# An order of two conversions at the start, and eight moves per weight tile spread over three groups

## The chip, the cores and the metric

One core of one Trainium2 chip runs the whole kernel. The metric is the device time of one execution in microseconds (us), the median of the timed runs.

## The reference

One decoder layer on 512 tokens of width 2048, in float32. Its input is multiplied by one wide weight; seven parts of the product go into a causal convolution of 31 taps with a layer norm and a gate, and into a forgetting attention of 16 heads with a gate. Both halves go through one output weight, and a residual with a layer norm ends it.

```python
z = jnp.einsum("bsd,de->bse", h, w_in) + b_in
glu_val, glu_gate, gate_c, q, k, v, f_logit, gate_a = _split_columns(z)
y_conv = _conformer_conv(glu_val, glu_gate, w_dw, b_dw, g_cn, b_cn)
y_conv = y_conv * jax.nn.silu(gate_c)
y_attn = _forgetting_attention(q, k, v, f_logit)
y_attn = y_attn * jax.nn.silu(gate_a)
y = jnp.concatenate([y_conv, y_attn], axis=-1)
sub = jnp.einsum("bse,ed->bsd", y, w_out) + b_out
h = _layer_norm(DN_ALPHA * h + sub, g_post, b_post)
```

## The kernel before

**Products.** Both large products are done in float32r with operands split into a high and a low half, three matmuls for one (`mm3`, lines 1081 to 1083), and by Strassen-Winograd's scheme: seven products of half-sized blocks instead of eight. A *group* g is 128 columns of two parts of the input product; there are 56, three for each of the 16 heads and 8 for the last gate. A group has seven *units* m of 24 matmuls each. They run in the order 1, 2, 5, 6, 3, 7, with unit 4 of a group in the third slot of the next one. So a step of the loop over (g, s) on each engine stands for one slot s of seven.

**Weights.** Of each group, SyncE (SP) loads four blocks of 512 KB into `raw` (`loads`, line 427): B11, B12, B21, B22. The seven units need B11, B21, B22, B12+B22 (unit 7, an adding DMA that GpSimd issues, `sum_3`, line 660, semaphore t3_in), B11+B12 (unit 5, `sum_1` on VectorE, line 1344, t1_done), that plus B22 (unit 6, `sum_2`, line 1352), and that plus B21 (unit 4, `sum_4`, an adding DMA, line 667, t4_in). For each unit n, ScalarE writes the high half (`high(n)`, line 801) and VectorE the low half (`low(n)`, line 1333) into one of three slots of `whl`; high(n) needs unit n-3 to be done.

**Start.** x is transposed on TensorE in quarters and sums of quarters, and split likewise by `x_high(f)` (ScalarE, line 808) and `x_low(f)` (VectorE, line 1379), four pieces of 512 columns each. Before the loop VectorE's order is low(0), a difference, low(1), a difference, sum_1(0), a difference (line 1403), low(2), x_low(3). ScalarE's is x_high(1), high(0), high(1), x_high(3), high(2), then three small copies of biases (lines 830 to 832). Unit n = 2 is group 0's unit 5, the third product that runs; it reads factor 3 of x. GpSimd's sum of x12 and x21 (line 717) waits for low_done 3, so for low(2).

**Sums of output weights.** The output product (behind group 55) needs, for each of 16 tiles k, four sums T1 to T4 of blocks of the output weight. They are built in DRAM (`t_dram`, 512 KB each) while the groups run: SP copies a block or an earlier sum (`copies`, `copy_sum`, line 482), and GpSimd adds another with an adding DMA (`out_sums`, `add_sum`, line 692). T1 and T3 start from w_out, T2 from a copy of the finished T1, T4 from a copy of the finished T2. Eight moves per tile. SP runs `loads(g)`, then `copies(g)`, then bias rows of the next head (four DMAs, line 510) and stores. `loads(g)` waits for low halves of groups g-2 and g-1, and, ahead of B22, for t3_in of g-1. So SP's step g is carried out while group g-1 is computed. GpSimd's step g is sum_3(g), masks, sum_4(g), out_sums(g).

**Other work.** VectorE carries the 31 taps of the convolution, some in each slot (`TAPS_AT`, and `TAPS_LAST` from group 48 on, line 1440). ScalarE's `evict` (line 867) takes unit 5 from PSUM behind the conversion of the same slot; TensorE's unit 3 waits for it. VectorE's eviction in slot 0 is line 1481; unit 4 waits for it.

Of the kernel before, what the change touches and what calls it, by code (L numbers as in the profile page):

```python
# [11 lines left out]
P = 128  # L12
SEQ = 512
D = 2048
# [3 lines left out]
HEADS = D // P  # L18
# [66 lines left out]
T1, T2, T3, T4 = range(4)  # L85
# [72 lines left out]
def build(nc, x, w_in, b_in, w_dw, b_dw, g_cn, b_cn, w_out, b_out, g_post, b_post, out, scratch):  # L158
# [3 lines left out]
    t_dram = nc.dram_tensor("out_sums_dram", (4, HEADS, P, 1024), F32).ap()  # L162
    ctx = ExitStack()
    with ctx:
# [205 lines left out]
        t_added = [sem(f"t{n + 1}_added") for n in range(4)]  # L370
# [52 lines left out]
        def _(sp):  # L423
# [57 lines left out]
            def copy_sum(t, k, src, copied):  # L481
                sp.dma_start(t_dram[t, k, :, :], src).then_inc(copied, 16)

            def copies(g):

                if g % 3 == 0 and 0 <= g // 3 - 2 < HEADS:
                    k = g // 3 - 2
                    sp.wait_ge(t_added[T1], 16 * (k + 1))
                    if k:
                        sp.wait_ge(t2_copied, 16 * k)  # L490
                    copy_sum(T2, k, t_dram[T1, k, :, :], t2_copied)
                if g % 3 == 1 and 0 <= g // 3 - 3 < HEADS:
                    k = g // 3 - 3
                    sp.wait_ge(t_added[T2], 16 * (k + 1))
                    if k:
                        sp.wait_ge(t4_copied, 16 * k)
                    copy_sum(T4, k, t_dram[T2, k, :, :], t4_copied)
                if g % 3 == 0 and 0 <= g // 3 - 1 < HEADS:
                    k = g // 3 - 1
                    if k:  # L500
                        sp.wait_ge(t13_copied, 32 * k)
                    copy_sum(T1, k, w_out[D + P * k:D + P * (k + 1), 0:1024], t13_copied)
                    copy_sum(T3, k, w_out[D + P * k:D + P * (k + 1), 1024:], t13_copied)

            def load_bias(h):

# [82 lines left out]
            g = GROUPS - 1  # L589
# [56 lines left out]
        def _(pool):  # L646
# [38 lines left out]
            def add_sum(t, k, src):  # L685
                if k:
                    pool.wait_ge(t_added[t], 16 * k)
                if t in (T1, T3):
                    pool.wait_ge(t13_copied, 32 * (k + 1))
                else:  # L690
                    pool.wait_ge(t2_copied if t == T2 else t4_copied, 16 * (k + 1))
                nc.gpsimd.dma_start(t_dram[t, k, :, :], src, accum_op=ALU.add).then_inc(t_added[t], 16)  # L692

            def out_sums(g):

                if g % 3 == 0 and 0 <= g // 3 - 1 < HEADS:
                    k = g // 3 - 1
                    add_sum(T1, k, w_out[D + P * k:D + P * (k + 1), 1024:])
                if g % 3 == 1 and 0 <= g // 3 - 1 < HEADS:
                    k = g // 3 - 1  # L700
                    row = P * CONV_ORDER[k]
                    add_sum(T3, k, w_out[row:row + P, 1024:])
                if g % 3 == 1 and 0 <= g // 3 - 3 < HEADS:
                    k = g // 3 - 3
                    row = P * CONV_ORDER[k]
                    add_sum(T4, k, w_out[row:row + P, 0:1024])
                if g % 3 == 2 and 0 <= g // 3 - 2 < HEADS:
                    k = g // 3 - 2
                    row = P * CONV_ORDER[k]
                    add_sum(T2, k, w_out[row:row + P, 1024:])  # L710
# [50 lines left out]
        def _(act):  # L761
# [17 lines left out]
            def high(n):  # L779

                if n not in UNIT_OF:
                    out_high(OUT_OF[n])
                    return
                g, m = UNIT_OF[n]
                if m == 1:
                    act.wait_ge(block_in[B11][g % 2], parity(g))
                elif m == 2:
                    act.wait_ge(block_in[B21][g % 2], parity(g))
                elif m == 3:
                    act.wait_ge(block_in[B22][g % 2], parity(g))  # L790
                elif m == 4:
                    wait_t4(act, g)
                elif m == 5:
                    act.wait_ge(t1_done, g + 1)
                elif m == 6:
                    act.wait_ge(t2_done, g + 1)
                else:
                    act.wait_ge(t3_in[g % 2], parity(g))
                if n >= 3:
                    act.wait_ge(unit_done, n - 2)  # L800
                nc.scalar.activation(w_high(n), source(n), ACT.Copy).then_inc(high_done, 1)  # L801

            def x_high(f):

                at_f = 4 * X_ORDER.index(f)
                for b in range(4):
                    act.wait_ge(xt_turned, X_BANKS if f == 2 else at_f + b + 1)
                    nc.scalar.activation(xh[:, f, 2 * b:2 * b + 2, :].rearrange("p k t -> p (k t)"), ps[:, x_bank(at_f + b), :],
                                         ACT.Copy, scale=-1.0 if f == 6 else 1.0).then_inc(xh_done, 1)
# [14 lines left out]
            x_high(1)  # L824
            high(0)
            high(1)
            x_high(3)
            high(2)
            act.wait_ge(rows_turned, 1)
            nc.scalar.activation(cols[:, :], ps[:, R5, 0:7 * HEADS], ACT.Copy).then_inc(cols_done, 1)  # L830
            nc.scalar.activation(cn[:, :], ps[:, R5, P:P + 3 * HEADS], ACT.Copy).then_inc(cols_done, 1)
# [1055 lines left out]
```

## Time and profile before

| | us |
|---|---|
| median of the timed runs | 1575.6 |
| all three | 1576.14, 1575.6, 1575.55 |
| the profiled execution | 1574.57 |
| its span, first to last instruction | 1572.8 |
| TensorE busy in it | 1549.7 |
| VectorE busy | 1445.4 |
| ScalarE busy | 840.9 |
| GpSimd busy | 250.3 |

PE is TensorE's matmuls, DVE VectorE, ACT ScalarE, POOL GpSimd, SP SyncE; "SPq" is SP's queue, whose instructions wait for semaphores and issue DMAs. L801 is line 801 of the kernel. Matmuls are pipelined, so the duration of one is longer than its share of the engine, and the starts tell the rate. An engine's idle time costs nothing unless TensorE comes to wait for it.

### The profile page before, as it was taken

Reading aid. Unit: us, or ns where it says so; the run is one execution under the profiler, and the core shown is the slowest. Engines: PE = TensorE matmul, PEld = TensorE weight load, DVE = VectorE, ACT = ScalarE, POOL = GpSimd, SP = SyncE. Lnnn points to the kernel's source line nnn. Section 1 sums busy time; section 2 is a strip of 40 time slices with the busy share of each in tenths; the row PEclk is TensorE's granted clock in tenths of the full one; section 3 lists DMA queues with packets and bytes.
Section 4 is the critical chain, followed back from the end, with each engine's and each line's share of the span. In section 5 each row is a group of like instructions: output and inputs, shape, how many; then the busy total and the mean of one; then the engine's idle time right before and its main releaser. Section 6 shows DMA issues by size and latency. Waiting matters only on the chain.

```text
span 1572.8 us, 29452 instructions
## 1 busy us (share of the span) xinstructions
PE 1549.7 (99%) x11574; PEld 1486.9 (95%) x11574; DVE 1445.4 (92%) x1975; ACT 840.9 (53%) x1225; POOL 250.3 (16%) x275
## 2 busy tenths in 40 slices
PE   7999999999999999999999999999999999999997
PEld 6999999999999999999999999999999988888886
DVE  7779999999999999999999999999989889986787
ACT  4565454554545545455454554545456676644462
POOL 1111212122121221212212122121110000000000
PEclk9999999999999999999999999999999999999999
DMA  8588888999999999999999999999899899888876
GB/s 226 127 204 190 222 204 215 234 211 241 224 226 229 213 241 223 231 217 223 239 219 232 223 220 238 230 224 219 196 278 287 245 345 340 297 235 249 259 211 204
DMA packets 316473, 365.23 MB, mean 232 GB/s; under 512 B 14561, under 2 KB 254337, under 8 KB 315025
## 3 DMA queue, kind: packets, MB, share of 16 engines
q1 hardware_dynamic: 285024, 259.93, 53.7%
q0 software_dynamic: 26784, 98.58, 35.0%
q10 hardware_dynamic: 4528, 4.85, 0.9%
q8 instruction: 92, 1.51, 0.4%
q14 instruction: 45, 0.37, 0.1%
HBM read 287.25 MB, written 87.06 MB: 238 GB/s over the span
## 4 chain that ended last, share of the span: by engine, by line
PE 90%; DVE 7%; issue 1%; DMA 1%; ACT 1%; SPq 0%; DVEq 0%; ACTq 0%
PE ps L1081 29%; PE ps L1083 29%; PE ps L1082 29%; DVE whl L1333 2%; DVE c_tiles L1440 1%; PE ps L1198 1%; DMA f_raw<-in_w_in_dram 1%; DVE raw L1352 1%; DMA raw<-in_w_out_dram 1%; PE ps L1192 0%; PE ps L1147 0%; ACT whl L801 0%; DVE xl L1379 0%; DVE raw L1344 0%; DVE res L1827 0%
## 5 line engine op out<-in xcount | busy, mean ns | idle before, releaser
L1081 PE MATMUL ps<-xh,whl 128*128 128x256 f32 x3136 | 894.4, 285 | 3.9 <-DVE xl L1379 1.4
L1083 PE MATMUL ps<-xh,whl 128*128 128x256 f32 x3136 | 887.7, 283 | 0.0
L1082 PE MATMUL ps<-xl,whl 128*128 128x256 f32 x3136 | 887.6, 283 | 0.0
L801 ACT ACTIVATE whl<-raw 128x1024 fp32r<-128x1024 f32 x392 | 415.3, 1061 | 555.2 <-PE ps L1083 474.6
L1081 PEld LDWEIGHTS ps<-xh,whl 128*128 128x128 f32 x3136 | 599.5, 191 | 5.9 <-issue 2.2
L1082 PEld LDWEIGHTS ps<-xl,whl 128*128 128x128 f32 x3136 | 599.7, 191 | 0.5 <-issue 0.5
L1083 PEld LDWEIGHTS ps<-xh,whl 128*128 128x128 f32 x3136 | 599.5, 191 | 0.0
L1333 DVE TENSOR_TENSOR whl<-raw,whl 128x1024 fp32r<-128x1024 f32 x392 | 477.5, 1218 | 52.4 <-ACT whl L801 52.4
L1440 DVE SCALAR_TENSOR_TENSOR c_tiles<-ps,taps,c_tiles 128x511 f32<-128x511 f32 (+14 forms) x480 | 349.9, 729 | 6.7
L660 POOL DMA_DIRECT2D raw<-raw x56 | 49.4, 883 | 558.3 <-DMA raw<-in_w_in_dram 452.1
L1081 PE MATMUL ps<-whl,yh 128*128 128x512 f32 x320 | 124.8, 390 | 1.3 <-issue 0.9
L1336 DVE TENSOR_TENSOR whl<-raw,whl 128x1024 fp32r<-128x1024 f32 x80 | 97.7, 1222 | 30.0 <-ACT whl L777 29.8
L1083 PE MATMUL ps<-whl,yl 128*128 128x512 f32 x320 | 124.6, 389 | 0.0
L1082 PE MATMUL ps<-whl,yh 128*128 128x512 f32 x320 | 124.6, 389 | 0.0
L777 ACT ACTIVATE whl<-raw 128x1024 fp32r<-128x1024 f32 x80 | 84.6, 1057 | 74.3 <-PE ps L1083 72.7
L667 POOL DMA_DIRECT2D raw<-raw x51 | 43.3, 848 | 319.9 <-DVE whl L1333 319.9
L1352 DVE TENSOR_TENSOR raw<-raw 128x1024 f32<-128x1024 f32 x56 | 73.8, 1319 | 1.9
L1081 PEld LDWEIGHTS ps<-whl,yh 128*128 128x128 f32 x320 | 60.1, 188 | 14.6 <-DVE whl_more L1336 1.7
L1083 PEld LDWEIGHTS ps<-whl,yl 128*128 128x128 f32 x320 | 60.1, 188 | 12.5
L1082 PEld LDWEIGHTS ps<-whl,yh 128*128 128x128 f32 x320 | 60.1, 188 | 12.4
L692 POOL DMA_DIRECT2D out_sums_dram<-in_w_out_dram x64 | 69.2, 1208 | 0.0
L1344 DVE TENSOR_TENSOR raw<-raw 128x1024 f32<-128x1024 f32 x56 | 68.2, 1218 | 0.0
(197 smaller groups left out, 1540.0 us busy)
## 6 DMA issues: line engine op xcount, KB each, us to landing
raw<-in_w_in_dram SPq DMA_DIRECT2D x224, 512.0 KB, 8.0
raw<-raw POOLq DMA_DIRECT2D x107, 512.0 KB, 6.0
out_sums_dram<-in_w_out_dram POOLq DMA_DIRECT2D x64, 512.0 KB, 9.6
raw<-out_sums_dram SPq DMA_DIRECT2D x64, 512.0 KB, 5.1
raw<-in_w_out_dram SPq DMA_DIRECT2D x48, 512.0 KB, 5.6
out_sums_dram<-in_w_out_dram SPq DMA_DIRECT2D x32, 512.0 KB, 9.4
out_sums_dram<-out_sums_dram SPq DMA_DIRECT2D x32, 512.0 KB, 9.7
x<-in_x_dram SPq DMA_DIRECT2D x8, 512.0 KB, 8.0
```

Of the source, the lines that this page charges most:

```text
L660: nc.gpsimd.dma_start(raw[:, ring(g, B12), :], raw[:, ring(g, B22), :], accum_op=ALU.add) \
L692: nc.gpsimd.dma_start(t_dram[t, k, :, :], src, accum_op=ALU.add).then_inc(t_added[t], 16)
L777: nc.scalar.activation(out_w(u, 0), raw_out(u), ACT.Copy).then_inc(high_done, 1)
L801: nc.scalar.activation(w_high(n), source(n), ACT.Copy).then_inc(high_done, 1)
L1081: nc.tensor.matmul(o, ah, bh, start=start, stop=False, skip_group_check=True)
L1082: nc.tensor.matmul(o, ah, bl, start=False, stop=False, skip_group_check=True)
L1083: return nc.tensor.matmul(o, al, bh, start=False, stop=True, skip_group_check=True)
L1333: vec.tensor_tensor(w_low(n), source(n), w_high(n), ALU.subtract).then_inc(low_done, 1)
L1336: vec.tensor_tensor(out_w(u, 1), raw_out(u), out_w(u, 0), ALU.subtract).then_inc(low_done, 1)
L1344: vec.tensor_tensor(raw[:, ring(g, SUM), :], raw[:, ring(g, B11), :], raw[:, ring(g, B12), :], ALU.add).then_inc(t1_done, 1)
L1352: vec.tensor_tensor(o, o, raw[:, ring(g, B22), :], ALU.add).then_inc(t2_done, 1)
L1440: vec.scalar_tensor_tensor(out=o[:, n:], in0=ps[:, U_BANK, 0:SEQ - n], scalar=tap, in1=o[:, n:], op0=ALU.mult, op1=ALU.add) \
```

## The change

Two things. On ScalarE, the conversion of unit 2's weights, high(2), is put ahead of the conversion of x's factor 3, x_high(3). And the eight moves of a tile are spread anew. Copies on SP in the steps g = 0, 1, 2 modulo 3 were T2, T1, T3 / T4 / none, and are T4, T2 / T3 / T1. GpSimd's additions were T1 / T3, T4 / T2 and are T1 / T4 / T3, T2. T1's copy of tile k now stands in step 3k+2 instead of 3k+3, T3's in 3k+4 instead of 3k+3, T4's in 3k+9 instead of 3k+10; T3's addition in 3k+5 instead of 3k+4. The semaphore of the copies of T1 and T3, which is shared, is waited for at 16 and 32 above each tile's start instead of 32.

```diff
             def copies(g):
 
+                if g % 3 == 0 and 0 <= g // 3 - 3 < HEADS:
+                    k = g // 3 - 3
+                    sp.wait_ge(t_added[T2], 16 * (k + 1))
+                    if k:
+                        sp.wait_ge(t4_copied, 16 * k)
+                    copy_sum(T4, k, t_dram[T2, k, :, :], t4_copied)
                 if g % 3 == 0 and 0 <= g // 3 - 2 < HEADS:
                     k = g // 3 - 2
                     sp.wait_ge(t_added[T1], 16 * (k + 1))
                     if k:
                         sp.wait_ge(t2_copied, 16 * k)
                     copy_sum(T2, k, t_dram[T1, k, :, :], t2_copied)
-                if g % 3 == 1 and 0 <= g // 3 - 3 < HEADS:
-                    k = g // 3 - 3
-                    sp.wait_ge(t_added[T2], 16 * (k + 1))
-                    if k:
-                        sp.wait_ge(t4_copied, 16 * k)
-                    copy_sum(T4, k, t_dram[T2, k, :, :], t4_copied)
-                if g % 3 == 0 and 0 <= g // 3 - 1 < HEADS:
+                if g % 3 == 1 and 0 <= g // 3 - 1 < HEADS:
                     k = g // 3 - 1
+                    sp.wait_ge(t13_copied, 32 * k + 16)
+                    copy_sum(T3, k, w_out[D + P * k:D + P * (k + 1), 1024:], t13_copied)
+                if g % 3 == 2 and g // 3 < HEADS:
+                    k = g // 3
                     if k:
                         sp.wait_ge(t13_copied, 32 * k)
                     copy_sum(T1, k, w_out[D + P * k:D + P * (k + 1), 0:1024], t13_copied)
-                    copy_sum(T3, k, w_out[D + P * k:D + P * (k + 1), 1024:], t13_copied)
...
                 if t in (T1, T3):
-                    pool.wait_ge(t13_copied, 32 * (k + 1))
+                    pool.wait_ge(t13_copied, 32 * k + (16 if t == T1 else 32))
...
                     add_sum(T1, k, w_out[D + P * k:D + P * (k + 1), 1024:])
-                if g % 3 == 1 and 0 <= g // 3 - 1 < HEADS:
+                if g % 3 == 2 and 0 <= g // 3 - 1 < HEADS:
                     k = g // 3 - 1
                     row = P * CONV_ORDER[k]
                     add_sum(T3, k, w_out[row:row + P, 1024:])
...
             high(1)
+            high(2)
             x_high(3)
-            high(2)
```

## Rows read from the trace of the kernel before

**Rows 1.** The page, span and part 1: busy us, share, instructions.

```profile
span 1572.8 us, 29452 instructions
PE 1549.7 (99%) x11574; PEld 1486.9 (95%) x11574; DVE 1445.4 (92%) x1975; ACT 840.9 (53%) x1225; POOL 250.3 (16%) x275
```

**Rows 2.** Busy time by stage (PE PEld DVE ACT POOL); then clock, DMA share, GB/s.

```profile
50.00:1100.00 1050.00, 1050.00 (x8659) 1045.70 (x8658) 997.19 (x1413) 553.82 (x856) 213.88 (x232) 1.00 0.93 220
1100.00:1160.00 60.00, 57.98 (x472) 56.89 (x471) 57.22 (x70) 26.51 (x35) 9.77 (x10) 1.00 0.92 227
```

**Rows 3.** Timeline of ACT at the start: start, us, instruction, idle before.

```profile
24.12 2.06 ACT L808 ACTIVATE xh<-ps 128x512 fp32r<-128x512 f32 x4 [6.39 <-PE ps L1147]
26.05 1.08 ACT L801 ACTIVATE whl<-raw 128x1024 fp32r<-128x1024 f32 x1
```

**Rows 4.** Timeline of DVE in the same stretch.

```profile
22.57 1.22 DVE L1344 TENSOR_TENSOR raw<-raw 128x1024 f32<-128x1024 f32 x1
23.70 2.28 DVE L1403 SCALAR_TENSOR_TENSOR x<-x 128x2048 f32<-128x2048 f32 x1
27.16 1.23 DVE L1333 TENSOR_TENSOR whl<-raw,whl 128x1024 fp32r<-128x1024 f32 x1 [1.17 <-ACT whl L801]
28.30 2.48 DVE L1379 TENSOR_TENSOR xl<-ps,xh 128x512 fp32r<-128x512 f32 x4
30.70 3.50 DVE L1352 TENSOR_TENSOR raw<-raw 128x1024 f32<-128x1024 f32 x1
```

**Rows 5.** Timeline of PE there.

```profile
29.13 0.35 PE L1081 MATMUL ps<-xh,whl 128*128 128x256 f32 x1 [1.44 <-DVE xl L1379]
...
34.95 0.52 PE L1147 MATMUL ps<-ident,x 128*128 128x128 f32 x3 [0.97 <-DVE xl L1379]
```

**Rows 6.** Timeline of POOL there.

```profile
28.54 4.58 POOL L717 TENSOR_TENSOR x<-x 128x2048 f32<-128x2048 f32 x1 [2.23 <-DVE whl L1333]
```

**Rows 7.** Timeline of PE in group 50.

```profile
1144.20 0.39 PE L1081 MATMUL ps<-xh,whl 128*128 128x256 f32 x1 [1.06 <-ACT p L867]
```

**Rows 8.** ACT at that moment; then, of its waits over the span (us, times, longest), one.

```profile
1142.73 1.06 ACT L801 ACTIVATE whl<-raw 128x1024 fp32r<-128x1024 f32 x1 [3.11 <-DMA raw<-raw]
...
ACT whl L801 <- DMA raw<-in_w_in_dram: 4.8, 2, 4.0
```

**Rows 9.** Timeline of POOL in groups 49 and 50.

```profile
1119.20 2.01 POOL L692 DMA_DIRECT2D out_sums_dram<-in_w_out_dram  x2
1134.27 0.88 POOL L660 DMA_DIRECT2D raw<-raw  x1 [13.07 <-DMA raw<-in_w_in_dram]
```

**Rows 10.** Landing times: L660 at 1134.27, L427 at 1121.4, the pair of L692 at 1119.20.

```profile
DMA to landing us min/median/max: 8.4/8.4/8.4
...
DMA to landing us min/median/max: 12.3/12.3/12.3
...
DMA to landing us min/median/max: 9.1/10.9/12.7
```

**Rows 11.** Timeline of DVE in group 50.

```profile
1153.78 0.41 DVE L1481 TENSOR_TENSOR tiles<-p,ps 128x256 f32<-128x256 f32 x1
```

**Rows 12.** Timeline of POOL in group 26.

```profile
612.84 1.16 POOL L692 DMA_DIRECT2D out_sums_dram<-in_w_out_dram  x1
```

**Rows 13.** Timeline of SP's queue, steps 27 and 28.

```profile
615.11 1.49 SPq L482 DMA_DIRECT2D out_sums_dram<-out_sums_dram  x1
...
627.17 9.80 SPq L427 DMA_DIRECT2D raw<-in_w_in_dram  x4
```

**Rows 14.** Landing times of L692, all 64.

```profile
DMA to landing us min/median/max: 8.2/9.6/12.7
```

**Rows 15.** L660 of group 28: issue, and time to landing.

```profile
L660 POOL DMA_DIRECT2D raw<-raw x1: 893/893/893, 644.9 to 644.9; - x1
...
DMA to landing us min/median/max: 10.5/10.5/10.5
```

**Rows 16.** Timeline of ACT, group 28, unit 7.

```profile
658.20 1.06 ACT L801 ACTIVATE whl<-raw 128x1024 fp32r<-128x1024 f32 x1 [1.46 <-PE ps L1083]
```

## The prediction

> **What bounds the kernel now.** I read the page's busy shares first [rows 1]: TensorE (PE) works 1549.7 of 1572.8 us, VectorE (DVE) 1445.4. A kernel with an engine at 99% gains only where that engine still stands still, 23.1 us in all, so the next view is the busy time by stage [rows 2]. The reader is to see how little of it lies where work flows: from 50 to 1100 us PE is busy all of 1050.00 us, from 1100 to 1160 it idles 2.02. The rest is the start and the tail. Matmuls are pipelined and their ends are modelled, so a busy PE could hide small gaps; but the starts follow each other at 0.12 us wherever I looked, a unit of 24 every 2.88. DMA is another matter: its share is 0.93 from 50 to 1100 [rows 2]. The moves of the change use that resource, so they can hurt nearly everywhere and can help only where PE waits.
>
> Then PE's timeline at its waits: 1.44 us at 29.13, for DVE's low halves of x [rows 5], and 1.06 at 1144.20, for an eviction by ACT (L867) [rows 7]. The swap in ScalarE's (ACT) opening touches the first, the moves the second.
>
> **Edit 1, high(2) ahead of x_high(3).** DVE runs low(2) before x_low(3), while ACT runs x_high(3) before high(2), so DVE waits for the later of ACT's two. ACT idles 6.39 us until PE's transposes are there, converts x_high(3) from 24.12 to 26.18, and begins high(2) (L801) at 26.05 [rows 3]. The sum that high(2) reads is DVE's L1344, 22.57 to 23.79. DVE ends its subtraction at 23.70+2.28 = 25.98, idles 1.17, runs low(2) at 27.16 and x_low(3) at 28.30 [rows 4]. PE's unit 2 starts at 29.13, its earlier work having ended at 29.13-1.44 = 27.69 [rows 5].
>
> After the swap: high(2) starts at 23.8, as soon as its sum is there, and ends at 23.8+1.08 = 24.9. x_high(3) runs from about 24.85, its first quarter there at 25.4, its last at 24.85+2.06 = 26.9. DVE is busy with its subtraction until 25.98 anyway, so low(2) starts there, 1.17 earlier, and x_low(3) at 28.30-1.17 = 27.13, when its four inputs are there. PE starts at 29.13-1.17 = 27.96, still behind its earlier work. ACT's three small copies of biases follow x_high(3) and are through before that. Price: **-1.17**. The bounds are PE's gap, -1.44, and +0.75, if the later start of x_high(3) (24.87, not 24.12) came through; it would only if DVE were free at once, and it is not. I take the value that DVE's own idle time gives.
>
> What is late next? GpSimd (POOL) starts its sum of x12 and x21 behind low(2), at 28.54, and holds 4.58 us to 33.12 [rows 6]; DVE's L1352 takes 3.50 to 34.20 in that time [rows 4], then come the low halves that PE's next wait, 0.97 before 34.95, is for [rows 5]. This chain hangs on low(2) as well and moves by the same 1.17. From 50 us on PE has no gap that could swallow the gain [rows 2], so it reaches the end.
>
> **Edit 2, the moves.** Per tile there are still eight transfers of 512 KB: four copies by SyncE (SP, L482) and four additions by POOL (L692). By step modulo 3 SP had 3, 1, 0 and POOL 1, 2, 1; now SP has 2, 1, 1 and POOL 1, 1, 2. Nothing computes on the sums before 1250. POOL issues one in 1.16 us [rows 12] and is 16% busy [rows 1]: nothing. What matters is what they share the DMA engines with: 0.52 MB at the 220 GB/s of the busy stretch [rows 2] is 2.4 us each.
>
> *Where a stall goes.* At 1144.20 PE waited 1.06 for L867 [rows 7], the eviction that ACT runs behind a conversion, and that conversion waited 3.11 for the adding DMA raw<-raw of group 50 [rows 8]. POOL issued it at 1134.27, after 13.07 of waiting for the load of B22 [rows 9]; it took 8.4. That load took 12.3: it was issued at 1121.4, behind two additions (1119.20) that took 9.1 and 12.7 [rows 10]. Group 49 is 1 modulo 3, so one of the two, T3's, now goes to group 50. The second of the pair landed some 3.6+0.5 = 4.1 behind the first, so the load should land 3 to 4 earlier, and the raw<-raw as much and more, as it then goes ahead of the loads of group 51. It has to land 1.06 earlier for PE to lose nothing. Price: **-1.06**, bounds 0 and -1.2 (the restart of the array, 0.39 for the first matmul against 0.28, adds a little).
>
> Is DVE late next? PE needs DVE's L1481 of group 50 four units behind the one that starts at 1144.20, at 1144.20+4x2.90 = 1155.8, now 1154.75; L1481 ends at 1153.78+0.41 = 1154.19 [rows 11]. In time by 0.5.
>
> *Where a wait comes.* SP's copy of T4 moves one step forward, ahead of the copy of T2, and waits for the addition into T2 that POOL issued a group before. Take steps 26 and 27. SP reaches its copies at 615.11 [rows 13]. The addition to T2 is issued at 612.84; now T3's goes ahead of it by 0.5 [rows 12]. Additions take 8.2 to 12.7 us, 9.6 in the middle [rows 14]. So it lands between 621.5 and 626, and SP stands 6 to 11 us. Queued behind: the copy of T2, then the loads for group 28, which SP began at 627.17 in any case, as they wait for DVE's low [rows 13]. With two issues of up to 1.5 each these start between 627.2 and 629. So the wait is nearly covered in the queue; its second effect is that two copies, 4.8 us of transfer, stand in the DMA engines when those loads and the raw<-raw DMAs come. The tightest use behind it is that of group 28: issued at 644.9, took 10.5, landed at 655.4, used at 658.20 [rows 15, 16]: room 2.8, and 1.5 more before PE feels it (the late one of group 50 was needed when unit 5 ended, 4.1 before 1144.20, and came 1142.7-1140.1 = 2.6 late, for 1.06). One copy less stands there, against it. I take **0**, by the nearest row: in the whole stretch ACT waited once for 4.0 us for a load [rows 8], and PE lost nothing [rows 2]. Bounds 0 and, if each of 15 periods lost half a us, +7.5; below nothing is excluded, as PE is never idle there.
>
> *Group 51 and step 2.* The pair of additions now stands in group 50, with two copies instead of one behind the load of B22 of group 51; and T1's first copy goes to step 2, at about 70 us. Either can make one raw<-raw late as that of group 50 was: bounds 0 and +1.06 each. I take 0, since before group 51 the queue is emptier by what group 49 no longer adds, and in step 2 one copy of 2.4 us has to use up room like the 2.8 above.
>
> **The sum.** -1.17 - 1.06 = -2.2 on a span of 1572.8 (1570.6). The profiled execution's own time is 1574.57 (1.8 around the span), so 1572.3; the median of the timed runs is 1575.6, 1.0 above it, so **1573.3**.
>
> **Rivals.** (a) *The double addition only moves its stall.* It now stands at 2 modulo 3 and the transfer of the next group, 51, is late as that of 50 was: -1.17-1.06+1.06 gives 1574.4. For: the same pair, the same load behind it. Against: the queue is emptier there. In the Trainium skill, DMA: Bandwidth & Descriptors, section "Queues, rings and completion order", each DMA engine takes packets from its queues in turn, and each issuer has its own ring; by that, three, two and three is no even load, since POOL's ring still has its pair, and this rival is what it would give. No row here shows the turns. (b) *Slower: SP's wait for T2.* The copies, held until 625 instead of 615, meet the loads of the next group and the four bias loads behind them, and group 28's transfer lands late. It decides from 2.8+1.5 = 4.3 us later landing; at half a us for each of 15 periods, 1573.3+7.5 = 1580.8. For: DMA share 0.93, room 2.8. Against: the queue drains while SP waits, one copy less stands there, and the sum of bytes is the same. (c) *The swap brings nothing at the end*: PE's wait at 34.95 grows by what the one before loses, because POOL or a load holds it. 1574.4. Against: POOL itself starts behind low(2). (d) *More goes*: less DVE lag behind an earlier ACT removes the other 0.96 of the 2.02 between 1100 and 1160 [rows 2] too; 1572.3.
>
> **Chances.** Forecast 0.55, (a) 0.14, (b) 0.14, (c) 0.07, (d) 0.10. Range 1572.0 to 1577.5: it holds all but most of (b) and half of (d). A measurement can tell about 0.2%, 3.15 us, from no change: faster (below 1572.45) 0.17, from (d) and the edge of the forecast; slower (above 1578.75) 0.13 from (b); same 0.70.
>
> **What the profile after would show.** Edit 1 is right if ACT's first L801 behind its long idle comes at 23.8, ahead of L808, and PE's 1.44 shrinks to 0.2 or 0.3 with 0.97 left as it is. Edit 2 is right if L867 is gone from PE's waits and ACT's wait for raw<-raw near 1142 with it; (a) shows as the same wait some 20 us later; (b) as a new SP wait at L482 of some 8 to 10 us sixteen times (that it comes is forecast, that PE pays is not) with PE idle between 50 and 1100. What would make it wrong: any PE idle in that stretch beyond 1 us in sum, above all beside ACT waits for DMA in groups 1 modulo 3.

## The result and the profile after

The median of five runs is 1584.88 us (1581.87 to 1589.64), against 1575.55 us (1575.01 to 1576.14) for the kernel before; the ratio is 1.0065, with a 95% interval of 1.0054 to 1.0076. The forecast was 1573.3. The change makes the kernel 0.65% slower, and its runs lie 7.8 us apart instead of 1.1. The profiled execution took 1583.29 us, of which its span is 1581.5. The page of the changed kernel, for [rows 1]. From SP's copies on, line numbers are three higher than before: L804 is `high`, L1336 `low`, L1347 `sum_1`, L870 the eviction that was L867. L427 (the loads) and L482 (the copies) keep theirs.

```profile
span 1581.5 us, 29452 instructions
PE 1553.3 (98%) x11574; PEld 1487.1 (94%) x11574; DVE 1446.1 (91%) x1975; ACT 840.8 (53%) x1225; POOL 242.5 (15%) x275
```

The span grew by 8.7 us; only 5.1 of them are idle time of PE, and 3.6 stand in "busy". That time is no work, as the instructions are the same in number; it must be pauses that the modelled ends of the matmuls cover. So for a kernel in which PE is nearly always busy, the starts of the same matmul in the two traces must be compared, not the busy times alone. The busy time by stage, as in [rows 2]:

```profile
50.00:1100.00 1050.00, 1045.44 (x8585) 1038.35 (x8584) 990.52 (x1402) 549.12 (x850) 203.74 (x229) 1.00 0.91 218
1100.00:1160.00 60.00, 58.63 (x483) 58.09 (x482) 58.17 (x74) 27.32 (x37) 9.93 (x10) 1.00 0.92 211
```

PE idles 4.56 us in the stretch where it idled 0.00 before, at the same granted clock of 1.00. The start is what the forecast said. The timelines of ACT, DVE, POOL and PE there, for [rows 3 to 6]:

```profile
23.87 1.06 ACT L804 ACTIVATE whl<-raw 128x1024 fp32r<-128x1024 f32 x1 [6.09 <-DVE raw L1347]
24.84 2.04 ACT L811 ACTIVATE xh<-ps 128x512 fp32r<-128x512 f32 x4
...
25.96 1.22 DVE L1336 TENSOR_TENSOR whl<-raw,whl 128x1024 fp32r<-128x1024 f32 x1
27.09 2.48 DVE L1382 TENSOR_TENSOR xl<-ps,xh 128x512 fp32r<-128x512 f32 x4
...
27.33 4.60 POOL L720 TENSOR_TENSOR x<-x 128x2048 f32<-128x2048 f32 x1 [0.87 <-DVE whl L1336]
...
27.93 0.35 PE L1084 MATMUL ps<-xh,whl 128*128 128x256 f32 x1 [0.22 <-DVE xl L1382]
...
33.76 0.41 PE L1150 MATMUL ps<-ident,x 128*128 128x128 f32 x2 [0.99 <-DVE xl L1382]
```

The loss is in the loop. The views of what each engine waited for (instruction, what ended the wait, us in sum, times, longest) of SP, ACT and PE:

```profile
SPq L482 <- DMA out_sums_dram<-in_w_out_dram: 144.7, 15, 10.8
...
ACT whl L804 <- DMA raw<-in_w_in_dram: 82.0, 21, 6.9
ACT whl L804 <- DMA raw<-raw: 23.6, 11, 3.5
...
PE ps L1084 <- DVE parts L1496: 4.2, 5, 1.1
PE ps L1084 <- ACT p L870: 1.9, 1, 1.9
```

SP stands 9.6 us for T2's addition in each of 15 periods. ACT waits 82.0 us for loads of weights; before it was 4.8 in two waits [rows 8]. Each step on the way from SP's wait to PE can be read around group 16. First the three loads that SP issues in a row, B11, B12 and B21, in the changed kernel:

```profile
L427 SPq DMA_DIRECT2D raw<-in_w_in_dram x3: 392/574/4946, 362.8 to 364.0; - x3
...
  ACT whl L804: 5.4, 1
...
DMA to landing us min/median/max: 9.5/17.0/18.0
```

Then the same three in the kernel before:

```profile
L427 SPq DMA_DIRECT2D raw<-in_w_in_dram x3: 374/721/1585, 364.0 to 365.3; - x3
...
DMA to landing us min/median/max: 4.7/6.0/6.9
```

They are issued no later than before (from 362.8 on, before from 364.0), and two of them take some 11 us longer to land. Then the timelines of DVE, ACT and PE in the changed kernel:

```profile
380.40 1.22 DVE L1347 TENSOR_TENSOR raw<-raw 128x1024 f32<-128x1024 f32 x1 [1.61 <-issue]
...
382.02 2.01 ACT L804 ACTIVATE whl<-raw 128x1024 fp32r<-128x1024 f32 x2 [5.41 <-DMA raw<-in_w_in_dram]
...
402.96 0.68 DVE L1496 TENSOR_TENSOR parts<-tiles,parts 128x512 fp32r<-128x512 f32 x1
...
403.70 0.50 PE L1084 MATMUL ps<-parts 128*128 128x512 f32 x1 [1.11 <-DVE parts L1496]
```

B12 was issued at 363.28 and lands 17.0 later, at 380.3; DVE's sum_1 starts at 380.40, so it waited for it, though the view calls its idle "issue". B21, issued at 363.95, lands 18.0 later, at 382.0, and ACT's conversion starts at 382.02. VectorE, busy for 990.52 of the 1050 us of this stretch, can't make up what it lost: 20 us on, its L1496 (the low half of a head's queries, which the attention's products read, in the groups 1 modulo 3 alone) ends after PE needs it, and PE pays 1.11. There are five such waits (403.70, 537.10, 801.85, 935.74, 1068.48), 4.2 us in sum.

The shift of the same matmul between the two traces, in steps: -1.21 at 27.93; +1.26 at 403.70, +1.37 at 537.10, +0.85 at 801.85, +0.98 from 916 to 928, +1.33 at 935.74, +0.56 at 1068.48, and from +0.28 to +0.60 each at 469.95, 575.54, 603.64, 974 to 1002 and 1120.72; -1.23 at 1150.68 and +1.96 at 1173.74. In sum +7.9 of the 8.7 of the span; the rest is in steps too small to place. Taken by stretch, the shift is -1.18 at 350, +7.29 at 1100 and +8.70 at the end: the loop up to 1100 lost 8.5 us, of which PE's waits name 4.2. Around group 28, whose loads are shown below, PE loses nothing: the shift stays at +2.97 from 603.64 to 801.85.

### The profile page after: what moved, and what is told of

Its sections match the earlier page's. It is cut to its first block, busy times and chain, and to the rows that moved or that the text cites. A ratio compares the mean times of both kernels' runs of the same rounds, so it can differ in the third digit from the quotient of the medians.

```text
span 1581.5 us, 29452 instructions
## 1 busy us (share of the span) xinstructions
PE 1553.3 (98%) x11574; PEld 1487.1 (94%) x11574; DVE 1446.1 (91%) x1975; ACT 840.8 (53%) x1225; POOL 242.5 (15%) x275
## 4 chain that ended last, share of the span: by engine, by line
PE 54%; DVE 27%; DMA 11%; issue 6%; ACT 2%; DVEq 0%; SPq 0%; ACTq 0%; POOLq 0%
PE ps L1084 18%; PE ps L1086 17%; PE ps L1085 17%; DVE whl L1336 10%; DMA raw<-in_w_in_dram 10%; DVE c_tiles L1443 7%; DVE raw L1355 2%; ACT whl L804 2%; DVE raw L1347 1%; DVE tiles L1480 1%; DMA f_raw<-in_w_in_dram 1%; DMA raw<-raw 1%; DVE tiles L1484 1%; DMA raw<-in_w_out_dram 1%; PE ps L1201 0%
## 5 line engine op out<-in xcount | busy, mean ns | idle before, releaser
L804 ACT ACTIVATE whl<-raw 128x1024 fp32r<-128x1024 f32 x392 | 413.7, 1060 | 552.6 <-PE ps L1086 354.9
L1336 DVE TENSOR_TENSOR whl<-raw,whl 128x1024 fp32r<-128x1024 f32 x392 | 480.3, 1225 | 53.7 <-ACT whl L804 53.1
L1347 DVE TENSOR_TENSOR raw<-raw 128x1024 f32<-128x1024 f32 x56 | 68.2, 1218 | 3.9 <-issue 3.9
```

Source lines behind the costliest of these rows:

```text
L1336: vec.tensor_tensor(w_low(n), source(n), w_high(n), ALU.subtract).then_inc(low_done, 1)
L1347: vec.tensor_tensor(raw[:, ring(g, SUM), :], raw[:, ring(g, B11), :], raw[:, ring(g, B12), :], ALU.add).then_inc(t1_done, 1)
```

## The experiments

Each kernel's ratio is to the kernel before, run on the same chip; its medians there were 1575.78 (first four kernels), 1575.25 (the next four), 1576.54 (three) and 1574.95 (the last).

### The two edits apart

**swap_only**: the kernel before with the swap in ACT's opening alone.

```diff
             high(1)
+            high(2)
             x_high(3)
-            high(2)
```

> The kernel before with the swap of the two conversions alone; the moves stay 4, 3, 1. Both theories of the loss (SP's wait for the addition into T2; the pair of additions in the groups 2 modulo 3) say the swap has no part in it: PE's gap at 29 us shrinks from 1.44 to about 0.2, the whole chain is 1.2 earlier, 1575.6 - 1.2 = 1574.4. The rival that the swap shifts the phase of the loads and so costs gives 1577 or more.

Measured: 1573.67 (ratio 0.9988, 0.9979 to 0.9998), 2.1 less than before. The interval holds the -1.17 forecast. Its PE waits at the old place in group 50, if for 0.74 instead of 1.06, from the timeline:

```profile
1142.65 0.39 PE L1081 MATMUL ps<-xh,whl 128*128 128x256 f32 x1 [0.74 <-ACT p L867]
```

**moves_only**: the changed kernel with ACT's opening as before.

```diff
-            high(2)
             x_high(3)
+            high(2)
```

> The changed kernel with the two conversions in their old order; only the moves are changed. If swap and moves add up: the changed kernel's 1584.9 + 1.2 = 1586.1 (it scattered from 1581.9 to 1589.6, so 1582 to 1591). PE's gap at 29 us is 1.44 again, SP waits some 145 us in 15 times at its copies, PE has some 5 us of idle time between 200 and 1100. If they don't add up, it stays under 1580.

Measured: 1584.80 (1.0067, 1.0042 to 1.0091). All of the loss is in the moves. SP's wait is there (146.8 us in 15), and PE's five waits for L1496 (4.6 us).

### Is it T4's early copy, which must wait?

**exchanged**: still three, two and three moves, still all computed, but T4's and T3's copies stay where they were in the kernel before, in steps 1 and steps 0 modulo 3. T2's addition has then long landed when it is asked for (around group 28 it lands at 624.3, and the copy goes out at 635.57).

```diff
-                if g % 3 == 0 and 0 <= g // 3 - 3 < HEADS:
+                if g % 3 == 1 and 0 <= g // 3 - 3 < HEADS:
                     k = g // 3 - 3
                     sp.wait_ge(t_added[T2], 16 * (k + 1))
...
-                if g % 3 == 1 and 0 <= g // 3 - 1 < HEADS:
+                if g % 3 == 0 and 0 <= g // 3 - 1 < HEADS:
                     k = g // 3 - 1
                     sp.wait_ge(t13_copied, 32 * k + 16)
```

> The changed kernel with T3's and T4's copies exchanged: T3's copy in steps 0 modulo 3, T4's in steps 1 modulo 3, a whole step behind T2's addition. Still 3, 2, 3 moves, all of it computed. Theory A: no SP wait at the copies, 1573 to 1575, and what the swap gives (1.2) and the stall of group 50 (1.06, unless it forms again in group 51) stay. Theory B: 1582 or more, as the additions are where they were.

Measured: 1573.13 (0.9983, 0.9973 to 0.9993), 11.7 less than the changed kernel. SP no longer waits at L482 at all, and ACT's wait for loads is back near what it was:

```profile
ACT whl L804 <- DMA raw<-in_w_in_dram: 5.1, 2, 3.9
```

So neither the even spread nor the pair of additions in steps 2 costs anything; the order T4 behind T2's fresh addition does.

**t4_of_t1**: the changed kernel, every move in its place, but T4's copy reads the finished T1. T4 then lacks its second block, so what the kernel returns is not the layer's output; the transfers are of the same number and size.

```diff
-                    sp.wait_ge(t_added[T2], 16 * (k + 1))
+                    sp.wait_ge(t_added[T1], 16 * (k + 1))
...
-                    copy_sum(T4, k, t_dram[T2, k, :, :], t4_copied)
+                    copy_sum(T4, k, t_dram[T1, k, :, :], t4_copied)
```

> The changed kernel, but T4 is copied from the finished T1 instead of T2, so that SP waits for an addition that landed groups before; places and sizes of all eight moves are unchanged. T4 then lacks the second block, so the fourth product's weights are not the right ones. Theory A (SP's wait holds the copies until they stand right ahead of the next group's loads): the wait is gone, the loads of B12 and B21 land in 6 to 10 us again instead of up to 18, 1573 to 1575. Theory B (the pair of additions in groups 2 modulo 3 and the spread itself are too much): it stays at 1582 to 1588.

Measured: 1573.17 (0.9984, 0.9975 to 0.9994). The same eight transfers by the same queues in the same steps are free once the dependency is gone: between 50 and 1100 the starts of PE keep their distance to those of the kernel before within 0.02 us, here and in `exchanged`. It is the time at which they go out that costs, not where they stand in the order.

### The wait itself, or what it holds back?

**bare_wait**: `exchanged`, and behind the copies of steps 0 SP waits for T2's addition without holding any copy.

```diff
+                if g % 3 == 0 and 0 <= g // 3 - 3 < HEADS:
+                    sp.wait_ge(t_added[T2], 16 * (g // 3 - 2))
```

> The kernel 'exchanged' (1573.1) with a bare wait of SP for the addition into T2 at the end of steps 0 modulo 3, behind the two copies, which go out on time. SP stands about as long as in the changed kernel (9.6 us each, 145 in sum). If the copies that the wait holds are what does harm, because they stand ahead of the next group's loads: nothing lost, 1572.5 to 1574.5. If it is SP that comes late to its loads: 1578 or more.

Measured: 1574.37 (0.9992, 0.9982 to 1.0001), against 0.9983 for `exchanged`. That is 1.2 us by the medians and 1.4 by the ratios, of the 11.7, and the intervals overlap; in its trace, too, the starts of PE keep theirs between 50 and 1100. In this kernel the wait ends before the loads could go anyway: around group 28 the addition lands at 624.51, and the first load is issued at 625.91.

**t2c_first**: the changed kernel with T2's copy ahead of the wait, so that one copy is held instead of two.

```diff
-                    copy_sum(T4, k, t_dram[T2, k, :, :], t4_copied)
...
                     copy_sum(T2, k, t_dram[T1, k, :, :], t2_copied)
+                if g % 3 == 0 and 0 <= g // 3 - 3 < HEADS:
+                    k = g // 3 - 3
+                    sp.wait_ge(t_added[T2], 16 * (k + 1))
...
+                    copy_sum(T4, k, t_dram[T2, k, :, :], t4_copied)
```

> The changed kernel (1584.9) with T2's copy, which waits for nothing fresh, ahead of T4's on SP. One copy is held instead of two. If harm goes with the number of copies held: much of it gone, B21 of groups 1 modulo 3 takes some 12 us instead of 16 to 18, PE's idle time in 200 to 1100 near 0, 1574 to 1578. If one held copy is enough: 1580 or more.

Measured: 1575.34 (0.9999, 0.9990 to 1.0009). SP's and ACT's waits:

```profile
SPq L482 <- DMA out_sums_dram<-in_w_out_dram: 129.1, 15, 9.7
...
ACT whl L804 <- DMA raw<-in_w_in_dram: 23.6, 7, 5.0
```

A wait of 8.6 each in front of one copy costs 2.2 us against `exchanged`; the changed kernel's, 9.6 each in front of two, costs nearly 12.

**t2_first**: the changed kernel, but GpSimd issues T2's addition ahead of T3's.

```diff
-                if g % 3 == 2 and 0 <= g // 3 - 1 < HEADS:
...
-                    add_sum(T3, k, w_out[row:row + P, 1024:])
...
                     add_sum(T2, k, w_out[row:row + P, 1024:])
+                if g % 3 == 2 and 0 <= g // 3 - 1 < HEADS:
...
+                    add_sum(T3, k, w_out[row:row + P, 1024:])
```

> The changed kernel with T2's addition ahead of T3's on POOL in groups 2 modulo 3. It lands some 3 us earlier, so SP stands 6 to 7 us instead of 9.6 and the two held copies go out that much earlier, ahead of the loads. Theory A: the loss goes down by half or more, 1574 to 1579. If the length of the wait has no part: 1582 or more.

Measured: 1573.07 (0.9987, 0.9978 to 0.9997). Two copies are held here as well, and each wait is 2.5 us shorter:

```profile
SPq L482 <- DMA out_sums_dram<-in_w_out_dram: 107.6, 15, 8.8
...
ACT whl L804 <- DMA raw<-in_w_in_dram: 16.8, 6, 3.9
```

SP's queue around group 28 of this kernel, and of the changed one behind it:

```profile
620.22 1.11 SPq L482 DMA_DIRECT2D out_sums_dram<-out_sums_dram  x2
626.13 4.02 SPq L427 DMA_DIRECT2D raw<-in_w_in_dram  x3
```

```profile
628.14 1.11 SPq L482 DMA_DIRECT2D out_sums_dram<-out_sums_dram  x2
630.55 5.68 SPq L427 DMA_DIRECT2D raw<-in_w_in_dram  x3
```

In both the loads start nearly on time: in the changed kernel at 630.55, against 627.17 before [rows 13], where its matmuls run 2.97 us behind, so 0.4 late; in `t2_first` at 626.13, its matmuls running 1.29 ahead, so 0.25 late. What differs is how far ahead of them the pair of copies begins to go out: 5.9 us or 2.4.

**wait_only**: the kernel before with the swap and with T4's copy a step earlier, ahead of all others. Four copies are held.

```diff
+                if g % 3 == 0 and 0 <= g // 3 - 3 < HEADS:
+                    k = g // 3 - 3
+                    sp.wait_ge(t_added[T2], 16 * (k + 1))
...
+                    copy_sum(T4, k, t_dram[T2, k, :, :], t4_copied)
...
-                if g % 3 == 1 and 0 <= g // 3 - 3 < HEADS:
...
-                    copy_sum(T4, k, t_dram[T2, k, :, :], t4_copied)
```

> The kernel before with the swap (1573.7) and T4's copy alone put one step forward: 4, 2, 1 moves plus the copy in steps 0, so five moves there and SP's wait ahead of four copies. T2's addition goes alone in its group and lands some 10 us after its issue. Theory A: four copies held behind a wait of about 6 to 8 us, ahead of the loads: as slow as the changed kernel or slower, 1582 to 1600. If the wait needs the pair of additions to do harm: under 1577.

Measured: 1583.68 (1.0053, 1.0038 to 1.0068).

```profile
SPq L482 <- DMA out_sums_dram<-in_w_out_dram: 103.2, 15, 7.9
...
ACT whl L801 <- DMA raw<-in_w_in_dram: 66.9, 16, 6.3
```

The wait is shorter than that of `t2_first` (6.9 against 7.2 each), and the kernel is 10.6 us slower: the length of the wait alone doesn't set the price; what it holds counts too, and how near to the loads that goes out.

### Place in SP's queue, or bytes?

**behind_loads**: T4's and T2's copies are issued by SP behind B21 of the next step and ahead of B22, so that the loads never stand behind them.

```diff
                 load_block(g, B21, 1, 0)
+                held_copies(g - 1)
```

> The changed kernel with the copies of T4 and T2 carried out by SP behind the next step's loads of B11, B12 and B21, ahead of B22, instead of ahead of all four. They go out at about the same time as in the changed kernel (some 625 to 630 us in groups 27 and 28), at a point where T2's addition has landed, so SP doesn't stand. If harm comes from their place ahead of the loads in SP's ring: gone, 1573 to 1575. If it comes from the bunch of transfers at that moment, whatever the order: 1579 or more.

Measured: 1590.50 (1.0095, 1.0080 to 1.0109), the slowest of all. The theory that the loads suffer because they stand right behind the copies in SP's queue falls. The copies of step 27 go out at 640.21 and 644.21, some 12 us later than was meant (the expectation had 625 to 630), so this run moves their time as well as their place. The loads of group 28, ahead of them, are well (8.1, 9.4 and 10.3 us), and those of group 29 are not, though they are issued from 658.1 on, when the two copies have landed (650.3 and 652.3). ACT's waits in this kernel:

```profile
ACT whl L808 <- DMA raw<-in_w_in_dram: 80.6, 15, 7.2
ACT whl L808 <- DMA raw<-raw: 40.0, 18, 3.4
```

and the landings of group 29's three loads:

```profile
DMA to landing us min/median/max: 10.2/11.5/17.5
```

The late load has only moved from groups 1 modulo 3 to groups 2 modulo 3.

**t3c_early**: the changed kernel with T3's copy moved into steps 0, ahead of the wait, into the stretch that the wait leaves emptier. From the issue of B22 to that of the next B11, 12.5 us, the changed kernel moves 2.44 MB in the middle of its groups 1 modulo 3, and `exchanged` 2.92; the DMA share there is 0.92 against 1.00, so it is not idle. T4's and T2's are held as in the changed kernel.

```diff
+                if g % 3 == 0 and 0 <= g // 3 - 1 < HEADS:
+                    k = g // 3 - 1
+                    sp.wait_ge(t13_copied, 32 * k + 16)
+                    copy_sum(T3, k, w_out[D + P * k:D + P * (k + 1), 1024:], t13_copied)
                 if g % 3 == 0 and 0 <= g // 3 - 3 < HEADS:
...
-                if g % 3 == 1 and 0 <= g // 3 - 1 < HEADS:
-                    k = g // 3 - 1
```

> The changed kernel with T3's copy in steps 0 modulo 3, ahead of SP's wait, instead of in steps 1; T4's and T2's copies are still held by the wait for some 9 us, and still stand ahead of the next group's loads. 4, 1, 3 moves. Theory C (the moves that the wait keeps out of the stretch behind the load of B22 have to go into the rest of the period, which is full; what counts is how many bytes move in that stretch): one copy is back in it and one is out of the rest, as in 't2c_first' (1575.3): 1573.5 to 1577. Theory D (two copies held right ahead of the loads of groups 1 modulo 3 do the harm, whatever else moves): 1582 or more, with the load of B21 there still at 15 us or more.

Measured: 1582.38 (1.0048, 1.0030 to 1.0065), 7.4 us more than the kernel before.

```profile
SPq L482 <- DMA out_sums_dram<-in_w_out_dram: 128.9, 15, 9.6
...
ACT whl L804 <- DMA raw<-in_w_in_dram: 45.1, 13, 6.4
```

It moves 2.96 MB in that stretch, as much as `exchanged`, and gives back 2.5 us of about 12 by the medians, with intervals that overlap (the changed kernel's is 1.0054 to 1.0076). Group 28's loads are as late as in the changed kernel (9.2, 10.4 and 16.2 us, there 8.6, 10.0 and 14.8), so what was missing is not bytes in that stretch. Of the two theories of the expectation D fits and C doesn't.

### A better order

**pair_only**: the swap, and of the moves only T3's addition from groups 1 to groups 2 modulo 3.

```diff
-                if g % 3 == 1 and 0 <= g // 3 - 1 < HEADS:
+                if g % 3 == 2 and 0 <= g // 3 - 1 < HEADS:
                     k = g // 3 - 1
                     row = P * CONV_ORDER[k]
                     add_sum(T3, k, w_out[row:row + P, 1024:])
```

> The kernel before with the swap (1573.7) and T3's addition alone moved to groups 2 modulo 3, so 4, 2, 2 moves; all copies stay. It tells the term of the stall apart: if the pair of additions in group 49 made the late raw<-raw of group 50, PE's 1.06 at about 1143 is gone, and some 0.1 to 0.8 comes back in group 51: 1572.6 to 1573.4. If the stall hangs on something else: 1573.7 with the wait as it was.

Measured: 1572.92 (0.9978, 0.9969 to 0.9987). PE's wait for L867 in group 50 is gone, and none stands in group 51. The step against `swap_only` (1573.67, on another chip) is 0.8 us by the medians, 1.6 by the ratios, and within the intervals; the forecast was 1.06. From 1100 to 1160 PE works 59.00 us instead of 57.98 [rows 2]:

```profile
1100.00:1160.00 60.00, 59.00 (x482) 57.91 (x481) 57.53 (x70) 26.63 (x35) 8.22 (x9) 1.00 0.91 223
```

**exchanged_t2_first**: `exchanged`, with T2's addition ahead of T3's on GpSimd.

```diff
-                if g % 3 == 2 and 0 <= g // 3 - 1 < HEADS:
...
-                    add_sum(T3, k, w_out[row:row + P, 1024:])
...
                     add_sum(T2, k, w_out[row:row + P, 1024:])
+                if g % 3 == 2 and 0 <= g // 3 - 1 < HEADS:
...
+                    add_sum(T3, k, w_out[row:row + P, 1024:])
```

> Both cures: T3's and T4's copies exchanged, and T2's addition ahead of T3's. Nothing waits for the earlier landing now, so it adds nothing to 'exchanged': 1573.1, 1572.5 to 1573.7. More gain would need PE idle time that neither has touched (0.95 for DVE's L1481 in groups 48 and 49).

Measured: 1572.82 (0.9979, 0.9970 to 0.9987); its fastest and slowest runs are 1571.98 and 1573.77. It computes everything, and is 0.21% faster than the kernel before and so some 0.8% faster than the changed one. It can't be told from `pair_only`, so the even spread itself brings nothing that shows.

### The experiments side by side

For each kernel, worked out from the issues and landings in its trace, over the 45 groups 10 to 54: how many copies SP's wait holds; how long ahead of the load of B11 of a group 1 modulo 3 the last of the copies of steps 0 goes out; the median time from issue to landing of B21 in groups 0, 1 and 2 modulo 3; and how many of the 45 loads of B21, and of the 90 of B11 and B12, took over 13.4 us, a cut set by hand. Behind them ACT's waits for loads, by how much the starts of PE moved against the kernel before between 50 and 1100, and the median time.

| kernel | held | ahead by | B21, groups 0 / 1 / 2 | late B21 | late B11, B12 | ACT waits | starts moved | median |
|---|---|---|---|---|---|---|---|---|
| before | 0 | 10.3 | 9.7 / 7.1 / 9.5 | 1 | 0 | 4.8 | 0 | 1575.6 |
| exchanged | 0 | 10.9 | 6.8 / 9.5 / 9.5 | 1 | 0 | 5.1 | 0.0 | 1573.1 |
| bare_wait | 0 | 11.0 | 7.0 / 9.6 / 9.5 | 1 | 0 | 9.1 | 0.0 | 1574.4 |
| t4_of_t1 | 0 | 10.9 | 6.7 / 9.3 / 9.5 | 5 | 0 | 17.7 | 0.0 | 1573.2 |
| pair_only | 0 | 8.9 | 7.0 / 10.0 / 10.2 | 7 | 0 | 20.3 | 0.0 | 1572.9 |
| t2_first | 2 | 4.4 | 6.7 / 10.0 / 9.7 | 4 | 0 | 16.8 | 0.0 | 1573.1 |
| t2c_first | 1 | 2.5 | 7.0 / 10.1 / 9.4 | 5 | 0 | 23.6 | 0.7 | 1575.3 |
| t3c_early | 2 | 2.0 | 6.7 / 15.5 / 8.2 | 10 | 4 | 45.1 | 5.4 | 1582.4 |
| wait_only | 4 | 3.2 | 9.4 / 14.6 / 8.9 | 15 | 6 | 66.9 | 9.2 | 1583.7 |
| moves_only | 2 | 1.9 | 7.0 / 11.3 / 9.6 | 10 | 4 | 67.6 | 7.1 | 1584.8 |
| changed | 2 | 2.0 | 6.8 / 14.8 / 13.0 | 14 | 4 | 82.0 | 8.5 | 1584.9 |
| behind_loads | 0 | behind it | 7.0 / 10.2 / 16.2 | 14 | 3 | 80.6 | 16.2 | 1590.5 |

The kernels fall in two classes. Up to 7 late loads of B21 cost nothing or 2 us; with 10 or more, and with the first late loads of B11 or B12, the time is 1582 or more. `swap_only` and `exchanged_t2_first` have 2 and 1 late loads of B21 and belong to the first class.

How a late load reaches PE shows when B12 of each group 1 modulo 3 is put beside PE's wait for DVE's L1496 (L1493 in some kernels) 39 to 41 us behind the load's issue. In the changed kernel:

| group | 10 | 13 | 16 | 19 | 22 | 25 | 28 | 31 | 34 | 37 | 40 | 43 | 46 |
|---|---|---|---|---|---|---|---|---|---|---|---|---|---|
| B12 took, us | 10.4 | 9.6 | 17.0 | 9.5 | 15.6 | 9.1 | 10.0 | 9.5 | 11.8 | 9.8 | 16.8 | 9.6 | 10.8 |
| PE waited, us | 0 | 0 | 1.11 | 0 | 1.10 | 0 | 0 | 0 | 0.58 | 0 | 1.08 | 0 | 0.31 |

The same over `before`, `exchanged`, `t2c_first`, `moves_only`, `t3c_early`, `wait_only` and the changed kernel, 91 groups: in 21 B12 took 10.8 us or more, and PE waited in all of them, 0.26 to 1.11 us; in 70 it took 10.6 or less, and PE waited in one (group 34 of `wait_only`, 10.2 and 1.10). No wait of that kind stands anywhere else in these seven. In the kernel before, the slowest of the 13 took 8.9. A late B21 alone costs PE nothing that shows: in groups 10, 28 and 37 of the changed kernel it took 16.0, 14.8 and 15.7 us with B12 at 10.4 or less, and no start of PE moved before the next group with a late B12. So the room of B12 is about 10.7 us from issue to landing, and the kernel before was some 2 us from it, on a load at which the forecast had not looked. `behind_loads` has such waits too (4.8 us in six), but at groups whose B12 took 9.6 or less: there what is late is another load. Which groups are late differs from kernel to kernel; that this is chance would also explain why the five runs of the changed kernel lie 7.8 us apart, which no trace of the other four shows.

## Why the prediction was wrong, point by point

**The swap: right.** ACT's first conversion behind its long idle was forecast at 23.8 and stands at 23.87; DVE's low(2) at 25.98, and stands at 25.96; PE's unit at 27.96, and stands at 27.93 with a wait of 0.22 (forecast 0.2 to 0.3). The same matmul is 1.21 earlier where -1.17 was forecast. PE's next wait stays at 0.99, so rival (c) did not happen. `swap_only` agrees.

**The stall of group 50: right in itself.** With T3's addition gone from group 49, L867's wait disappears; in `pair_only`, where this is the only move, it doesn't come back in group 51 either (some 0.1 to 0.8 was expected there). In the changed kernel it does, and larger. The timelines of POOL, ACT and PE there:

```profile
1148.10 2.01 POOL L695 DMA_DIRECT2D out_sums_dram<-in_w_out_dram  x2
1162.70 0.88 POOL L663 DMA_DIRECT2D raw<-raw  x1 [12.59 <-issue]
...
1172.27 1.06 ACT L804 ACTIVATE whl<-raw 128x1024 fp32r<-128x1024 f32 x1 [3.39 <-DMA raw<-raw]
...
1173.74 0.39 PE L1084 MATMUL ps<-xh,whl 128*128 128x256 f32 x1 [1.89 <-ACT p L870]
```

This is rival (a), which gave it 1.06; it measured 1.89. With it the term that was forecast at -1.06 came out as -1.23 + 1.96, some +0.7. The pair of additions alone is not its cause, since `pair_only` and `exchanged` have the same pair and no such wait, and `t4_of_t1` and `bare_wait` have 0.2 and 0.5. It is larger only where copies are held close ahead of the loads (`t2c_first` 0.82, `moves_only` 1.17, here 1.89); `t2_first`, which holds two for less long, has none. What makes it there is not shown further.

**The wait of SP: its size right, its price wrong.** This is the step that failed. The text forecast that SP stands 6 to 11 us, and it stood 9.6; that the loads still start on time, and around group 28 they did within 0.4; and then: "The tightest use behind it is that of group 28 ... I take **0**". The starts of PE say what this term was: +8.5 us between 50 and 1100, and nothing in `exchanged` and `t4_of_t1`. Two things in the step were wrong.

The first is which use is the tightest. The room of 2.8 + 1.5 us was that of the adding DMA raw<-raw of group 28 [rows 15, 16], which in the changed kernel landed in time (PE's waits don't name it up to 1100, though ACT waits 23.6 us for such transfers over the span, 3.1 before). The loads of B12 and B21, the second and third behind the copies, were never looked at. They were taken to be safe once they are issued on time. In the middle of the groups 1 modulo 3 B21 takes 15 us instead of 7, and B12 is late with it at times; ACT's conversion hangs on the one, DVE's sum on the other, and it is the late B12 that PE's waits go with.

The second is what carries it to PE. The forecast looked for a late eviction by ACT (L867). What PE pays for, as far as its waits can be read, is DVE: it stands for B12, at 91% it has no room to catch up, and it ends its L1496 late, 40 us behind the loads. The sign of that was in the rows: DVE was busy 997.19 of the 1050 us up to 1100, and 57.22 of 60 from there to 1160 [rows 2].

Rival (b) named the mechanism, copies that are held until they meet the loads of the next group and the four bias loads, and gave 1580.8 at half a microsecond for each of 15 periods. Held copies that meet the next loads are what happened; what lands too late for PE is not the transfer of group 28 that it named, but B12 at some places. Its price was set by half a microsecond that no row gave. Measured against 1573.3 it is 11.6, or 0.77 for each period, with group 51's stall in it; the upper bound of 7.5 was too small as well. The chance of 0.14 rested on "the queue drains while SP waits": it does nearly drain (at 628.14, when the two copies are released, only the load of B22 is still out, until 629.44, and they land in 3.8 and 6.0 us), and that saved nothing. The sign that the text itself set for being wrong, PE idle in 50 to 1100 beyond 1 us beside ACT's waits for DMA in groups 1 modulo 3, came as 4.56 us; the SP wait came 15 times and not 16.

**What is shown of the cause.** The fresh dependency is it: without it the same moves in the same steps cost nothing (`t4_of_t1`, `exchanged`). The wait itself is not (`bare_wait`). Nor is it the place right ahead of the loads in SP's own queue (`behind_loads`), nor fewer bytes in the stretch of the wait (`t3c_early`). With two copies whose last goes out within about 2 us of the loads, or four whose last goes out 3.2 us ahead, or two behind them, 10 to 15 of 45 loads of B21 took over 13.4 us, where the kernels without such copies have 1 to 7; in the worst third of the groups B21 takes 14.6 to 16.2 us in the middle, in `moves_only` 11.3. One copy 2.5 us ahead (`t2c_first`) costs 0.7 us of PE's starts in the loop.

**What stays open** is why the landing of one load grows by 5 us or more where another of the same kind doesn't, and how the part of the loss that stands in no wait of PE's comes about (4.3 of the 8.5 us in the loop; it falls in small steps behind late groups, and there is none of it in `exchanged`, `bare_wait`, `t4_of_t1`, `pair_only` and `t2_first`). The two classes fit one reading. GpSimd issues the raw<-raw of `sum_4` (t4's) and T1's addition some 5.5 us behind the loads. In the changed kernel they go out at 637.12 and 637.67, while B21 of group 28 (issued at 631.66) hasn't landed; t4's lands at 644.68, ahead of B21 at 646.41, though issued 5.5 us later. In `t2_first` B21 lands at 637.23, ahead of t4's 639.57. A load that isn't finished when these two come would then share the DMA engines with them, and land later. The Trainium skill, in DMA: Bandwidth & Descriptors, section "Queues, rings and completion order", says that a DMA engine with work in several rings takes a packet from each in turn. By that a load has to share with what another issuer adds later. The landings out of the order of issue agree with that; that the turns are the cause was not tried, and in `t2_first`, where B21 lands before t4's too, the overlap is 4.5 us all the same. No run moved GpSimd's two transfers alone.

## What to carry to other kernels

A copy that is issued one step earlier but depends on a transfer that was only just begun doesn't go out earlier: its queue holds it, and everything behind it, until just before the next loads. Before such a move, look at when its source is finished, and then at the landing of each load behind it and at its first reader, not only at the wait that stalls today. And where the second engine has no room (here VectorE, 997 of 1050 us), a late operand on it is paid for by the first one, some 20 us after the second has waited, and at another line.

## What the runs showed of the hardware that was not expected

A copy within DRAM of 512 KB is no fixed term. The page's rows of transfers (KB each, median us from issue to landing) for the same 32 copies, of before and of the changed kernel:

```profile
out_sums_dram<-out_sums_dram SPq DMA_DIRECT2D x32, 512.0 KB, 9.7
```

```profile
out_sums_dram<-out_sums_dram SPq DMA_DIRECT2D x32, 512.0 KB, 4.9
```

Released behind SP's wait, with at most one load of SP still out where it was looked at (group 28), they land in half the time, while the third load behind them takes twice as long in the middle (14.8 against 7.1 us); the median over all 224 loads went only from 8.0 to 8.9 us, which hides that one load.

The issue of a transfer has no fixed price either. In the kernel before, SP's own instruction for a copy from the output weight takes 0.6 to 1.7 us, all 32 times. In the changed kernel the one for T3's copy takes 2.9 to 7.7 us in eight of the groups 1 modulo 3, just those whose B21 took 14.8 us or more, and 0.8 to 1.6 in the other eight. In group 16, where the loads of B12 and B21 are unfinished, it is 6.03:

```profile
374.33 6.03 SPq L482 DMA_DIRECT2D out_sums_dram<-in_w_out_dram  x1
```
